# Six-layer transformer block on one core: where activation halves begin in on-chip memory

## What is computed

```
y_a = chunked_spatial_gating(gelu(gm_u), gelu(gm_v), ...)
y_b = mamba2_mixer(ssm_z, ssm_xbc, ssm_dt, ...)
y_c = diff_attention(da_q, da_k, da_v, ...)
g = sigmoid(gates).reshape(bsz, s, 3, D_MODEL)
merged = g[:,:,0]*(y_a @ w_branch_a) + g[:,:,1]*(y_b @ w_branch_b) + g[:,:,2]*(y_c @ w_branch_c)
x = x + merged @ w_out
h = rmsnorm(x); up = causal_dwconv(h @ ffn_w_up); gate, val = split(up)
x = x + (silu(gate) * val) @ ffn_w_down
```

## Time and profile before

| what | value |
|---|---|
| three runs, median (lowest to highest) | 2358.95 us (2358.03 to 2360.83) |
| profiled execution, span from the first to the last instruction | 2357.0 us |
| TensorE matmul busy | 2318.0 us (98%), 15,344 matmuls |
| VectorE, ScalarE, GpSimd busy | 1455.3, 1305.4, 334.5 us |
| HBM traffic | 398.93 MB, mean 169 GB/s |

### The profile page before, as it was taken

One profiled execution on the slowest core, in us unless ns is written; L12 is line 12 of the kernel. 1 busy time (PEld: TensorE's weight loads), 2 busy tenths in 40 slices (PEclk: granted clock), 3 DMA queues, 4 the chain that ended last, 5 costly groups with the idle time before them and its releaser, 6 DMA issues.

```text
span 2357.0 us, 36716 instructions
## 1 busy us (share of the span) xinstructions
PE 2318.0 (98%) x15344; PEld 2077.0 (88%) x15344; DVE 1455.3 (62%) x2209; ACT 1305.4 (55%) x1958; POOL 334.5 (14%) x307
## 2 busy tenths in 40 slices
PE   7999999999999999999999999999999999999999
PEld 6799978888899888998789988899899898998998
DVE  6654555546654546556764577576687676765875
ACT  5554465555644556445564467464665675655654
POOL 0100032212100413001010003333000022530000
PEclk9999999999999999999999999999999999999999
DMA  6255543333455534555245544344455453444553
GB/s 266 90 213 182 181 175 143 142 128 125 180 196 183 194 142 163 186 196 201 100 179 190 186 176 159 137 155 164 177 195 182 174 184 126 168 155 161 199 195 125
DMA packets 58181, 398.93 MB, mean 169 GB/s; under 512 B 6816, under 2 KB 7072, under 8 KB 11680
## 3 DMA queue, kind: packets, MB, share of 16 engines
q1 hardware_dynamic: 56864, 393.75, 46.0%
q10 hardware_dynamic: 1152, 2.83, 0.3%
HBM read 395.51 MB, written 1.05 MB: 168 GB/s over the span
## 4 chain that ended last, share of the span: by engine, by line
PE 89%; DVE 5%; ACT 4%; issue 1%; POOL 0%; DMA 0%; SPq 0%; ACTq 0%; DVEq 0%; POOLq 0%
PE b L1281 14%; PE b L1283 13%; PE b L1282 13%; PE b L1179 12%; PE b L1180 12%; PE b L1181 12%; PE b L1184 6%; PE b L1188 4%; DVE wlo L1929 2%; ACT b L1575 1%; ACT whi L1579 1%; PE b L1247 1%; PE b L1248 1%; DVE xb L2225 1%; PE b L1257 0%
## 5 line engine op out<-in xcount | busy, mean ns | idle before, releaser
L1929 DVE TENSOR_TENSOR wlo<-raw,whi 128x2048 fp32r<-128x2048 f32 x362 | 843.6, 2335 | 449.4 <-ACT whi L1579 449.1
L1579 ACT ACTIVATE whi<-raw 128x2048 fp32r<-128x2048 f32 x362 | 690.4, 1912 | 429.9 <-PE b L1283 233.6
L1281 PE MATMUL b<-xh,whi 128*128 128x256 f32 x2560 | 723.9, 283 | 0.6
L1283 PE MATMUL b<-xh,wlo 128*128 128x256 f32 x2560 | 712.6, 278 | 0.0
L1282 PE MATMUL b<-xl,whi 128*128 128x256 f32 x2560 | 712.0, 278 | 0.0
L1281 PEld LDWEIGHTS b<-xh,whi 128*128 128x128 f32 x2560 | 480.4, 188 | 5.3 <-DVE wlo L1929 2.8
L1282 PEld LDWEIGHTS b<-xl,whi 128*128 128x128 f32 x2560 | 481.4, 188 | 1.9
L1283 PEld LDWEIGHTS b<-xh,wlo 128*128 128x128 f32 x2560 | 481.2, 188 | 0.0
L1179 PE MATMUL b<-whi,xh 128*128 128x512 f32 x640 | 262.9, 411 | 1.4 <-DVE wlo L1929 1.4
L1179 PE MATMUL b<-whi,oh 128*128 128x512 f32 x656 | 259.0, 395 | 0.6 <-DVE ol L2216 0.6
L1180 PE MATMUL b<-wlo,oh 128*128 128x512 f32 x656 | 256.1, 390 | 0.0
(11 more groups left out here) (237 smaller groups left out, 2931.5 us busy)
## 6 DMA issues: line engine op xcount, KB each, us to landing
raw<-in_w SPq DMA_DIRECT2D x362, 1024.0 KB, 4.8
gt<-in_rows SPq DMA_DIRECT2D x8, 512.0 KB, 4.0
bt<-in_rows SPq DMA_DIRECT2D x8, 512.0 KB, 4.9
abq<-in_rows ACTq DMA_DIRECT2D x2, 768.0 KB, 6.3
x<-in_x SPq DMA_DIRECT2D x1, 1024.0 KB, 6.5
bc<-in_rows SPq DMA_DIRECT2D x4, 256.0 KB, 5.3
out<-x SPq DMA_DIRECT2D x4, 256.0 KB, 2.3
msk<-in_masks SPq DMA_DIRECT2D x1, 768.0 KB, 21.3
```

Source lines behind the costliest of these rows:

```text
L1281: pe.matmul(out, wh[:, k, cs], ah[:, kk, :], start=kk == 0 and s == 0, stop=False, skip_group_check=True)
L1283: last = pe.matmul(out, wl[:, k, cs], ah[:, kk, :], start=False, stop=final and k == 3, skip_group_check=True)
L1579: return ac.activation(out, i, ACT.Copy)
L1929: ve.tensor_tensor(B.wlo[r][:, :], B.raw[r][:, :], B.whi[s][:, :], ALU.subtract).then_inc(sem["loV"], 1)
```

## The change

No instruction is added, taken away or put in another place. What changes is where some data begin:

- The low half of activations 1, 3, 5, 7 to 11 begins at element 56 of `xl` in place of 24: remainder 224 in place of 96.
- `oh` and `ol` are now views into two slightly longer buffers. Their first views keep remainder 0 (`ol` begins 8 elements into a buffer whose address has remainder 224). Second views `yh` (56 elements into the first buffer) and `yl` (at the start of the second) have remainder 224; branch a, the second half of branch b, and branch c of the second mixers use these.
- `yq` begins 56 elements into a longer buffer: remainder 224.
- By the longer buffers, all that is declared after `ol` lies 256 bytes further (same remainder), and all that is declared after `yq` (`y`, `sigs`, `btok`, `small`, `wst`, `wdh`, `wdl` and smaller ones) 480 bytes further.

```diff
--- before.py
+++ after.py
@@ -1273,7 +1273,7 @@
         elif src[2] == 1 and half == 0:
             ah, al = B.yq[:, 0, :, :], B.yq[:, 1, :, :]
         else:
-            ah, al = B.oh, B.ol
+            ah, al = B.yh, B.yl
         out = B.bank[b][:, 256 * s:256 * s + 256]
         cs = slice(128 * block, 128 * block + 128)
         for k in range(4):
@@ -1716,7 +1716,7 @@
         b, n = use["opart", *key]
         blk = key[1]
         a.wait_ge(f"full{b}", n + 1)
-        copy(B.oh[:, 2 * blk:2 * blk + 2, :],
+        copy((B.oh if key[0] < 4 else B.yh)[:, 2 * blk:2 * blk + 2, :],
              B.bank[b][:, :].rearrange("p (k n) -> p k n", k=2)).then_inc(sem["ohi"], 1)
 
     def unturned(f):
@@ -1847,7 +1847,7 @@
 
     def ya_hi(l, j):
         a.wait_ge("yam", mark["yam", (l, j)])
-        copy(B.oh[:, 2 * j:2 * j + 2, :], B.sigs[0][:, 2 * j:2 * j + 2, :]).then_inc(sem["yahi"], 1)
+        copy(B.yh[:, 2 * j:2 * j + 2, :], B.sigs[0][:, 2 * j:2 * j + 2, :]).then_inc(sem["yahi"], 1)
 
     def z(l, q):
         for t in range(2):
@@ -1887,7 +1887,7 @@
     def yparts(l, t, q):
         b, n = use["yturn", l, t, q]
         g = B.colp(f"sng{l}")
-        to = B.oh[:, 4:8, :] if q else B.yq[:, 0, :, :]
+        to = B.yh[:, 4:8, :] if q else B.yq[:, 0, :, :]
         a.wait_ge(f"full{b}", n + 1)
         for k in range(4):
             kk = 4 * q + k
@@ -2197,8 +2197,9 @@
         b, n = use["opart", *key]
         blk = key[1]
         v.wait_ge("ohi", mark["ohi", key])
-        ve.tensor_tensor(B.ol[:, 2 * blk:2 * blk + 2, :], B.bank[b][:, :].rearrange("p (k n) -> p k n", k=2),
-                         B.oh[:, 2 * blk:2 * blk + 2, :], ALU.subtract).then_inc(sem[f"empty{b}"], 1)
+        oh, ol = (B.oh, B.ol) if key[0] < 4 else (B.yh, B.yl)
+        ve.tensor_tensor(ol[:, 2 * blk:2 * blk + 2, :], B.bank[b][:, :].rearrange("p (k n) -> p k n", k=2),
+                         oh[:, 2 * blk:2 * blk + 2, :], ALU.subtract).then_inc(sem[f"empty{b}"], 1)
 
 
 
@@ -2382,7 +2383,7 @@
     def ya_lo(l, j):
         sl = slice(2 * j, 2 * j + 2)
         v.wait_ge("yahi", mark["yahi", (l, j)])
-        ve.tensor_tensor(B.ol[:, sl, :], B.sigs[0][:, sl, :], B.oh[:, sl, :], ALU.subtract).then_inc(sem["yalo"], 1)
+        ve.tensor_tensor(B.yl[:, sl, :], B.sigs[0][:, sl, :], B.yh[:, sl, :], ALU.subtract).then_inc(sem["yalo"], 1)
 
     def head_roots(key, buf):
         n, width = B.heads_of(buf)
@@ -2434,7 +2435,7 @@
     def yparts(l, t, q):
         b, n = use["yturn", l, t, q]
         g, sl = B.colp(f"sng{l}"), slice(128 * t, 128 * t + 128)
-        h, to = (B.oh[:, 4:8, :], B.ol[:, 4:8, :]) if q else (B.yq[:, 0, :, :], B.yq[:, 1, :, :])
+        h, to = (B.yh[:, 4:8, :], B.yl[:, 4:8, :]) if q else (B.yq[:, 0, :, :], B.yq[:, 1, :, :])
         v.wait_ge("yhi", mark["yhi", (l, t, q)])
         for k in range(4):
             kk = 4 * q + k
@@ -2750,7 +2751,9 @@
         self.nsink = sb("nsink", [128, 32])
         self.rl = sb("rl", [128, 2, 16])
         self.og = several(3, "og", [128, 2, 512])
-        self.oh, self.ol = sb("oh", [128, 8, 256], F32R), sb("ol", [128, 8, 256], F32R)
+        self.out = sb("oh", [128, 2104], F32R), sb("ol", [128, 2056], F32R)
+        self.oh, self.ol = self.outs(0, 8)
+        self.yh, self.yl = self.outs(56, 0)
         self.v, self.qT = [sb("v0", [128, 2, 512])], [sb("qT0", [128, 4, 256])]
         self.kT = [sb("kT0", [128, 4, 256])]
         with ExitStack() as one:
@@ -2766,7 +2769,8 @@
         self.xb = sb("xb", [128, 12, 256])
         with ExitStack() as steps:
             self.xs = sb("xs", [128, 2, D], F32, steps)
-        self.yq = sb("yq", [128, 2, 4, 256], F32R)
+        yq = sb("yq", [128, 2104], F32R)
+        self.yq = yq[:, 56:2104].rearrange("p (h k n) -> p h k n", h=2, k=4)
         self.y = sb("y", [128, 2, D])
         self.sigs = several(2, "sigs", [128, 4, 256])
         self.btok = sb("btok", [128, 2, 128])
@@ -2813,8 +2817,11 @@
     def act(self, x):
 
 
-        places = (8, 0) if x in (0, 2, 4, 6) else (0, 24)
+        places = (8, 0) if x in (0, 2, 4, 6) else (0, 56)
         return [a[:, at:at + 2048].rearrange("p (k n) -> p k n", k=8) for a, at in zip(self.acts, places)]
+
+    def outs(self, *places):
+        return [a[:, at:at + 2048].rearrange("p (k n) -> p k n", k=8) for a, at in zip(self.out, places)]
 
     def cols_of(self, w):
         return [b.rearrange("p (k n) -> p k n", k=4) for b in (self.whi[w % NHL][:, :], self.wlo[w % NRAW][:, :])]
```

## The result

The changed kernel takes 2367.57 us (median of 6 runs) against 2358.97 us before: 8.6 us or 0.36% slower, ratio 1.0034 with a 95% interval of 1.0023 to 1.0044. One of the 6 runs took 10,969 us and is left out of the ratio. The profiled execution has a span of 2365.9 us, 8.9 us more than before.

What follows compares the result with a forecast made beforehand. The prediction took TensorE's successive matmuls to bound the kernel. Only the branches' 2.1 us counted, other terms being taken as nothing: 2358.95 - 2.1 = 2356.9 us, with a range from 2347 to 2362.5 us.

Steps and rivals of the forecast that it cites:

- sign of being wrong: Feed-forward runs of 96 column matmuls, forecast to stay at 11.13 us, changing by more than 0.1 us either way.
- the second part: 2560 low halves streamed by L1282, remainder 96 to 224: no change taken, bounds of 2.6 us either way.
- The second place that seemed to agree: Matmuls loading only 16 weight columns: xh 279 and 279 ns, xl 278 ns, read as 96 and 224 costing the same.
- The first part: 768 branch column matmuls, remainder 0 to 224 in all operands: 2.7 ns less each, 2.07 us less in all.
- The third part: 352 matmuls of 512 columns with the low half as stationary operand: no change taken, bounds of 1.5 us either way.
- Rival 2: Equal remainders cost: 7680 matmuls out of xh and xl go from 117.2 to 119.9 ns, 20.7 us more; chance 0.08.
- Rival 3: Equal remainders bring every column run to the slower 117.8 ns rhythm: 3.0 us more, 2362.0 us; chance 0.06.
- Rival 1: Equal remainders bring L1281 out of xh from 283 to 278 ns: 10.5 us less, 2346.4 us; chance 0.16.
- Rival 4: The branches' 2.7 ns comes from their surroundings, not the address: time stays at 2358.95 us; chance 0.08.

## Why the prediction was wrong

What bounds the kernel was read rightly: the branch stretches and the feed-forwards follow TensorE's step, and the sum of the steps gives the change to 0.1 us. The prediction's own sign of being wrong came up: the feed-forward runs went from 11.13 to 11.24 us.

The step that failed is the second part, the 2560 streamed low halves: "So 96 and 224 cost the same to within 1 ns, and I take nothing, with bounds of 1 ns x 2560 = 2.6 us either way." Measured alone it is 8.6 us. The fault lies in what was compared: the high half at 224 and the low half at 96 were both read inside the pair (224, 96), and the price was put on each stream by itself. The price belongs to the sequence of the three streams against the weights. With the low half at 224, L1282 rose by 3 ns, and so did L1283, which had not been touched. The second place that seemed to agree, with 16 columns of weights, couldn't carry it: it too was read inside the pair (224, 96), and with narrower products the pairs come in another order.

The first part, the branches, had the right sign and not the size: 2.07 us forecast, 1.2 measured in the steps. It gave (224, 224) the step of (224, 96), 117.2 ns, for the same reason; with the low half at 96 the forecast's gain comes about (117.1 ns, 768 x 2.8 = 2.2 us; 2356.8 us against 2359.1).

The third part, low halves as stationary operand, was taken at nothing, and for these that held: in the second layers the step of the 512-column matmuls with `xl` stationary went from 233.2 to 232.9 ns. The 1.4 us more of the 512-column steps came from others, above all from L1181 with `ol` stationary, 227.2 to 229.0 ns (574 steps, 1.0 us). `ol` kept its remainder there, and with the activations' low half alone moved it is 229.1 ns as well, so this too came with a neighbour's address; how is open.

Rival 2 had the side; its price of 20.7 us was too high, the branches did not stay at 119.9 ns as it said, and its reason, equal remainders as such, is refuted by (32, 32) at 116.7 ns. Rival 3 had one thing right: a set of addresses can have two rhythms. It was given 0.06 on the sight of one slow run, where it would have deserved a question: if addresses fixed the step, that run could not exist. But it doesn't account for the loss. It would have brought every run to 117.8 ns, and (224, 224) takes 118.3 in all the feed-forwards and in both long runs of the convolution inputs; a choice between rhythms wasn't seen there. Rival 1 is refuted: the step of L1281 fell by 0.6 ns and not by 4.1, and the others came up to it. Rival 4 is refuted by the branches.

So the cause is shown as far as this: the low half's address against that of the weights, in one line of code, sets the step of all three lines. Open stays the rule by which remainder, width of the product and beginning of a run give the step. Theories of own value, of spacing, of the load beside a stream and of its own weights all fell. That the weights' own address takes part is shown by the branches with the weights at remainder 32; how is not.

## What to carry to other kernels

When two operands differ in an address and in price, don't carry the price of one to the other: a step in a sequence of matmuls belongs to the whole sequence, so change one address in one stage and read every line of that stage. Where a long run of equal matmuls has more than one step length in a trace, look at how the runs begin before blaming the operands. A kernel with several alike stages can carry a scan, another setting in each stage, in one run, but what it reads holds for stages that begin alike.

## What was not expected of the hardware

Long runs of the column product sit at few levels, 113.4, 115.6, 116.7, 117.8 and 120.0 ns among them, and stay there for a hundred steps and more, at a mean granted clock of 0.996 to 1.000 of 2.4 GHz in all these traces. At (192, 192) a lead-in of 64 columns, whose own start is 0.03 us before the next one's, moves a run by 4.3 ns a step.

The Trainium skill, "TensorE: Matmul & The Clock Gate", section "Step-by-step: what each phase is for", says that matmul and weight load have read ports of their own, and that loading the next weights doesn't take bandwidth from the running matmul. The runs here don't agree with that, if it means that where and how wide the weights are loaded makes no difference to the matmuls: with the weights at remainder 32 and the streams where they were the branches' step went from 119.9 to 118.3 ns, and at (224, 224) the step is 118.3 ns with weights of 128 columns and 116.6 with 64. Whether it is bandwidth that is lost, no run here shows.
